# Stores of k and v straight from 32x32 blocks that VectorE has turned

## What is computed

```python
proj = xn @ w_in
u_a, z_a, q, k, v, z_b, g_a, g_b = jnp.split(proj, SPLITS, axis=-1)
y_a, h_last = s5_scan(u_a, h0, A_re, A_im, log_dt, B_re, B_im, C_re, C_im, D)
q = q.reshape(b, L, SB_HEADS, SB_HEAD_DIM)
k = k.reshape(b, L, SB_HEADS, SB_HEAD_DIM)
v = v.reshape(b, L, SB_HEADS, SB_HEAD_DIM)
o = sb_sweep(q, k_all, v_all, q_pos, k_pos, sb_bias).reshape(b, L, SB_WIDTH) * jax.nn.silu(z_b)
merged = jax.nn.sigmoid(g_a) * (y_a @ w_branch_a) + jax.nn.sigmoid(g_b) * (o @ w_branch_b)
return x + merged @ w_out, k, v, h_last
```

## Time and profile before

| | |
|---|---|
| median of the runs | 2971.93 us (2971.42 to 2975.23, 3 runs) |
| profiled execution, first to last instruction (span) | 2972.2 us; no other time of that execution is given |
| TensorE busy | 2927.0 us, 98% |
| VectorE busy | 1367.9 us, 46% |
| ScalarE busy | 1026.9 us, 35% |
| GpSimd busy | 433.7 us, 15% |
| mean granted clock of TensorE | 0.995 |
| DMA packets | 426099, of which 65122 under 512 bytes |

### The profile page before, as it was taken

The page is one execution under the profiler, slowest core; times in us unless marked ns, Lnnn a source line. Parts: engine busy times, 40 slices in busy tenths (PEclk is TensorE's granted clock), DMA queues, the critical chain, the costliest instruction groups (busy, mean ns, idle before and its releaser), DMA issues.

```text
span 2972.2 us, 48716 instructions
## 1 busy us (share of the span) xinstructions
PE 2927.0 (98%) x19148; PEld 2900.2 (98%) x19148; DVE 1367.9 (46%) x2579; ACT 1026.9 (35%) x1251; POOL 433.7 (15%) x1119
## 2 busy tenths in 40 slices
PE   6999999999999999999999999999999999999998
PEld 5999999999999999999999999999999999999997
DVE  6624453462445345244435524534566534422266
ACT  6235225423522541352253145125422421211242
POOL 7500330230032033004203300510000000000000
PEclk8999999999999999999999999999999999999999
DMA  6332332233233223323322331332448754332283
GB/s 185 84 107 70 85 90 88 74 92 104 65 93 99 84 67 89 100 65 99 105 72 71 92 106 52 103 100 72 150 154 300 244 189 138 114 112 71 82 244 114
DMA packets 426099, 329.05 MB, mean 111 GB/s; under 512 B 65122, under 2 KB 388274, under 8 KB 423858
## 3 DMA queue, kind: packets, MB, share of 16 engines
q1 hardware_dynamic: 425906, 326.34, 36.6%
HBM read 235.72 MB, written 73.73 MB: 104 GB/s over the span
## 4 chain that ended last, share of the span: by engine, by line
PE 90%; DMA 3%; SPq 2%; DVE 2%; ACT 1%; issue 1%; DVEq 0%; ACTq 0%
PE acc L1842 81%; PE side L1985 2%; PE side L2000 2%; DMA w_raw<-in_w_branch_a 1%; PE side L1809 1%; PE side L1980 1%; DMA t_sig_ga<-work 1%; PE side L1941 1%; SPq L522 0%; DMA work<-work 0%; PE side L1942 0%; PE side L2101 0%; DMA t_u_new<-work 0%; SPq L500 0%; DMA work<-in_x_prompt 0%
## 5 line engine op out<-in xcount | busy, mean ns | idle before, releaser
L1842 PE MATMUL acc<-x_high,w_high 128*128 128x344 f32 (+2 forms) x5440 | 1761.3, 324 | 3.8 <-DVE x_low L1421 2.0
L1842 PE MATMUL acc<-x_high,w_low 128*128 128x344 f32 (+2 forms) x5440 | 1734.6, 319 | 0.0
L1842 PE MATMUL acc<-x_low,w_high 128*128 128x344 f32 (+2 forms) x5440 | 1734.6, 319 | 0.0
L1842 PEld LDWEIGHTS acc<-x_high,w_high 128*128 128x128 f32 x5440 | 1023.4, 188 | 6.8 <-DVE x_low L1421 2.2
L1842 PEld LDWEIGHTS acc<-x_low,w_high 128*128 128x128 f32 x5440 | 1023.5, 188 | 1.0
L1842 PEld LDWEIGHTS acc<-x_high,w_low 128*128 128x128 f32 x5440 | 1022.4, 188 | 0.0
L1406 DVE TENSOR_TENSOR w_low<-w_raw,w_high 128x1024 fp32r<-128x1024 f32 x233 | 288.5, 1238 | 567.0 <-ACT w_high L930 564.3
L930 ACT CAST w_high<-w_raw 128x1024 fp32r<-128x1024 f32 x232 | 242.6, 1046 | 882.6 <-PE acc L1842 790.2
L1282 POOL COPY work<-s_tables 128x28 f32 x16 | 3.3, 206 | 1460.5 <-DVE work L1559 1208.3
L1559 DVE TENSOR_TENSOR work<-work,side 128x128 f32<-128x128 f32 x64 | 18.4, 287 | 319.9 <-PE side L1985 319.9
L986 ACT ACTIVATE work<-work 128x128 f32<-128x128 f32 (+3 forms) x64 | 43.9, 686 | 160.4 <-DVE work L1567 160.2
(11 more groups left out here) (320 smaller groups left out, 2560.0 us busy)
## 6 DMA issues: line engine op xcount, KB each, us to landing
w_raw<-in_w_in SPq DMA_DIRECT2D x160, 512.0 KB, 3.9
w_raw<-in_w_out SPq DMA_DIRECT2D x48, 512.0 KB, 4.0
work<-t_sig_ga SPq DMA_DIRECT2D x24, 516.0 KB, 4.0
out<-work SPq DMA_DIRECT2D x18, 512.0 KB
t_qk<-stage SPq DMA_DIRECT2D x16, 516.0 KB, 5.0
work<-t_qk SPq DMA_DIRECT2D x16, 516.0 KB, 4.7
t_sig_gb<-stage SPq DMA_DIRECT2D x16, 516.0 KB, 4.2
t_sig_ga<-stage SPq DMA_DIRECT2D x16, 516.0 KB, 4.7
```

The lines of the kernel that those rows point to most:

```text
L1842: ins = mm(acc[s][:, a, 0:n], w[b][:, kk, :], x[:, kx, c0:c0 + n], start=start, stop=stop)
```

## The change

Two instructions of VectorE turn k and v inside their stage buffers, each 32x32 block by itself (`V.transpose`). Afterwards partition 32q + a of block j holds features 32q to 32q + 31 of token 32j + a. `rows_out` stores that in four transfers, one for each q, each with 1024 runs of 32 floats (128 bytes), and the eight new tokens' columns in a fifth as 1024 single elements. The stores of k are issued in chunk 7, behind the second half's block loads, those of v in chunk 9. For q, ScalarE copies the eight new tokens' columns alone, and SyncE stores them as 1024 single elements in place of the tile. `attn_load` becomes one load, of v's rows, 512 bytes each, back from `v_prompt`. TensorE's three groups of transposes go, with their copies; the scores of the first block of queries wait for the load instead. The scratch tensor `t_qk` goes.

```diff
-                if t == Q:
-
-                    sp.wait_ge(at_in, i * 48 + PRIMED)
-                dst = {ZA: lambda: t_sza[bass.ds(i, 1)], Q: lambda: t_qk[0:1], K: lambda: t_qk[1:2], GB0: lambda: t_sgb[bass.ds(2 * i, 1)],
+                if t == Q:
+                    sp.dma_start(t_qs[:, bass.ds(i * P, P)].rearrange("b d -> d b"), stage[s][:, SEQ:TOK], allow_slow_non_contiguous=True).then_inc(stage_sent[s], 16)
+                    return
...
-                sp.wait_ge(stage_sent[0], i * 48 + 16 + PRIMED)
-                sp.wait_ge(stage_sent[1], i * 64 + 16 + PRIMED)
-                for n, dst in enumerate((qT, kT)):
-                    sp.dma_start(dst, t_qk[n]).then_inc(at_in, 16)
-                sp.wait_ge(stage_ready[0], i * 4 + 2 + PRIMED)
-                sp.dma_start(vT, stage[0][:, :]).then_inc(at_in, 16)
+                sp.wait_ge(kv_sent, i * 80 + 80 + PRIMED)
+                sp.dma_start(vtok.rearrange("p (b d) -> p b d", b=8),
+                             v_prompt[0, 0].rearrange("(b p) h d -> p b h d", p=P)[:, :, bass.ds(i, 1), :].rearrange("p b h d -> p b (h d)")).then_inc(at_in, 16)
+
+            def rows_out(turned, buf, rows, new, done):
+
+                sp.wait_ge(turned, i + 1)
+                for q in range(4):
+                    sp.dma_start(rows[0, 0][:, bass.ds(i, 1), q * 32:(q + 1) * 32].rearrange("(j a) h d -> a j (h d)", a=32),
+                                 buf[q * 32:(q + 1) * 32, 0:SEQ].rearrange("a (j d) -> a j d", d=32)).then_inc(done, 16)
+                sp.dma_start(new[0, :, 0, bass.ds(i, 1), :].rearrange("b h d -> (h d) b"), buf[:, SEQ:TOK], allow_slow_non_contiguous=True).then_inc(done, 16)
...
                 if cn == 7:
                     toeplitz(1)
+                    rows_out(k_turned, stage[1], k_prompt, k_sample, stage_sent[1])
+                if cn == 9:
+                    rows_out(v_turned, stage[0], v_prompt, v_sample, kv_sent)
...
-                if cn == 13:
-                    rows_out(vtok_ready, vtok, v_prompt)
-                    new_out()
-                if cn == 15:
-                    rows_out(ktok_ready, ktok, k_prompt)
...
-    VT, NTR, KTR, ZB_AT = 45, 46, 57, 44
+    K_TURN, V_TURN, ZB_AT = 26, 34, 44
...
             if t in (Q, K, V):
-                nc.scalar.copy(tok3(stage[s][:, :]), acc_v(t % 2)).then_inc(stage_ready[s], 1)
+                if t == Q:
+                    nc.scalar.copy(stage[s][:, SEQ:TOK], acc[t % 2][:, NB - 1, NC - NEW:NC]).then_inc(stage_ready[s], 1)
+                else:
+                    nc.scalar.copy(tok3(stage[s][:, :]), acc_v(t % 2)).then_inc(stage_ready[s], 1)
...
-                if p == KTR:
-                    dve.wait_ge(k_tr, i + 1)
-                    V.tensor_copy(ktok, side_flat).then_inc(ktok_ready, 1)
+                if p == K_TURN:
+                    dve.wait_ge(stage_ready[1], i * 4 + 1 + PRIMED)
+                    V.transpose(stage[1][:, 0:SEQ], stage[1][:, 0:SEQ]).then_inc(k_turned, 1)
+                if p == V_TURN:
+                    dve.wait_ge(stage_ready[0], i * 4 + 2 + PRIMED)
+                    V.transpose(stage[0][:, 0:SEQ], stage[0][:, 0:SEQ]).then_inc(v_turned, 1)
...
-                if p == VT:
-                    pe.wait_ge(at_in, i * 48 + 48 + PRIMED)
-                    pe.wait_ge(yt_ready, 2 * i + 2)
-                    for kb in range(8):
-                        last_op = tr(side_flat[:, kb * P:(kb + 1) * P], vT[:, kb * P:(kb + 1) * P], ident[:, :])
-                    last_op.then_inc(v_tr, 1)
-                if p == KTR:
-                    pe.wait_ge(z_ready, 8 * i + 4)
-                    for kb in range(8):
-                        last_op = tr(side_flat[:, kb * P:(kb + 1) * P], kT[:, kb * P:(kb + 1) * P], ident[:, :])
-                    last_op.then_inc(k_tr, 1)
-                if p == NTR:
-                    pe.wait_ge(vtok_ready, i + 1)
-                    for n, src in enumerate((qT, kT, vT)):
-                        last_op = tr(side[0:NEW, 0, n * P:(n + 1) * P], src[:, SEQ:TOK], ident[:, :])
-                    last_op.then_inc(new_tr, 1)
...
                         if qb == 0:
-                            pe.wait_ge(new_ready, i + 1)
+                            pe.wait_ge(at_in, i * 16 + 16 + PRIMED)
+                            pe.wait_ge(yt_ready, 2 * i + 2)
```

More of the change, by code:

```diff
@@ L227, in build @@
     c = Carve(work)
-    qT, kT, vT = c.take(TOK), c.take(TOK), c.take(TOK)
-    wT = vT[:, 0:SEQ]
+    c.at = 2 * TOK
+    wT = c.take(SEQ)
+    c.at = 3 * TOK
     vtok = c.take(SEQ)
     zb = [c.take(SEQ) for _ in range(2)]
-    ktok = c.take(SEQ)
+    c.at += SEQ
     lk, rl = c.take(SEQ), c.take(SEQ)
     szb = c.take(TOK)
-    smp = c.take(3 * P, NEW)
     c = Carve(work)
@@ L306, in build @@
         ("s5_hn_ready", "s5_ys_mm", "s5_ys_ready", "s5_yt_mm", "s5_yt_ready", "s5_y_sent", "s5_state_sent")]
-    at_in, v_tr, vtok_ready, k_tr, ktok_ready, new_tr, new_ready, kv_sent = [sem(s) for s in
-        ("attn_in", "v_tr", "vtok_ready", "k_tr", "ktok_ready", "new_tr", "new_ready", "kv_sent")]
+    at_in, k_turned, v_turned, kv_sent = [sem(s) for s in ("values_in", "k_turned", "v_turned", "v_sent")]
     sc_mm, z_ready, lr_ready, l_ready, arg_ready, w_ready, w_tr, wt_ready, pv_mm, oz_ready, oz_sent, szb_ready = [sem(s) for s in
@@ L363, in acc_v, with sent_before @@
         return acc[s][:, 0:banks, 0:n]
+    SENT = (48, 128)
+    def sent_before(t):
+        s, m = stage_of(t)
+        return 64 + 16 * m if s == 1 and m else 16 * m
     def tok3(ap):
@@ L573, in phase_a @@
                 ahead(cn)
-                if cn % 2 == 1 and cn > 1 and cn // 2 - 1 not in (U, V, ZB, GA0)[0:4 if last else 3]:
+                if cn % 2 == 1 and cn > 1 and cn // 2 - 1 not in (U, K, V, ZB, GA0)[0:5 if last else 4]:
                     send(cn // 2 - 1)
@@ L1011, in _ @@
             if f < 2:
[L1012 removed]
+                act.wait_ge(stage_sent[f], FT * SENT[f] + PRIMED)
             else:
```

31 lines of the change are left out of this document (6 added, 25 removed).

## The result

| | median, us | runs | ratio to before, 95% interval |
|---|---|---|---|
| before | 2972.41 | 2971.42 to 2975.23 | |
| after | 3204.57 | 3192.93 to 3211.89 | 1.0772 [1.0757, 1.0786] |
| forecast | 2955.5 (2952 to 2990) | | |

The change made the kernel 7.7% slower; the forecast said 0.6% faster, and its range did not hold the time. The profiled execution of after spans 3196.2 us, at a mean granted clock of 0.968.

The account below looks back on a forecast made before the run. TensorE, busy 2927.0 of 2972.2 us, was taken to bound the kernel. Removing 2.07 us of transposes in each of eight passes, with no stall, gave -16.6 us: 2955.5 us, range 2952 to 2990.

Parts of the forecast that it names:

- the landing of the swap: First swap of scan halves, queued behind k's stores, second pass: lands at 418.2 us, limit 419.2, so no stall.
- t: Time per packet of the short stores on the DMA queue: taken as 16 ns, bounds 9.4 and 47 ns.
- are cheaper than it up to 32 ns each: q's 1024 element stores, replacing a 516 KB store: claimed cheaper than that store up to 32 ns per element.
- The low bound: Low end of packet time for short stores: 9.4 ns from single-element loads, 10.4 ns from 64-byte loads; gives no stall.
- The term of the gain: Transposes taken off TensorE in the projection loop: 2.07 us per pass, 16.6 us over eight passes.
- The stores of rows: k's 128-byte runs on the DMA queue: 256 packets per engine, at 16 ns each, leaving 1.0 us before a stall.
- The readback of v: Load of v's rows before the scores: lands by 453.2 us, wanted at 460.8, 7.6 us to spare, cost nothing.
- Rival 1: Short stores at 32 ns delay the swap; TensorE waits 4.1 us per pass at step 36; 2988 us; chance 0.26.
- Rival 2: Stores at 23 to 27 ns; the stall gives back the transposes' gain; 2966 to 2976 us; chance 0.10.
- rival 4: VectorE's and ScalarE's score chain sets the pace of steps 47 to 79; removed work gives nothing; 2972 us; chance 0.03.
- Rival 3: v's readback lands late for the scores; 2 us beyond the margin leaves no gain, 2972 us; chance 0.03.
- The row I named for "wrong": Sign against the forecast: TensorE idle before step 36, released by VectorE, 4 us per pass or more; short packets above 25 ns.

Follow-up runs that it names:

- experiment 7: Changed kernel with q's and v's new tokens stored as 32-byte runs and k's 1024 elements sent to SBUF instead of memory: 2960.53 us, ratio 0.9948.
- experiment 1: Changed kernel with the three single-element stores of new tokens written as 128 runs of 32 bytes, in another order: 2958.67 us, ratio 0.9948.
- experiment 6: Changed kernel, q's and v's new tokens in 32-byte runs, k's store made 1024 runs of 32 bytes, 512 bytes apart in scratch: 2960.07 us, ratio 0.9950.
- experiment 8: Changed kernel with the same three element stores moved later, to groups 13, 15 and 17, from a small tile: 2967.01 us, ratio 0.9972.
- experiment 3: Kernel before, complete, with three stores per pass of 1024 single elements to scratch added at groups 5, 7 and 9: 3202.64 us, ratio 1.0768.

## Why the prediction was wrong

**The step that failed** is the landing of the swap, 409.7 + 0.32 t + 1.8 + 0.3 + 1.3, and with it the sentence on q, "are cheaper than it up to 32 ns each". Both price a store by the time its packets hold the engines. t was on the safe side: 13.0 to 13.7 ns for the rows and 9.2 ns for the elements, both below the 16 ns I took. (The 23 ns I read from the earlier trace rows for the 256-byte store was a misreading: the trace has 60 packets of 256 bytes there at 16 ns each, and 60 of 4 bytes that also took time.) By that formula there was no stall. But the 1.3 us from the last packet to the end, and the 28 ns for each packet behind, came from rows in which no element store stands ahead. Behind one, the packets took 363 ns and the swap 18.00 us. The 32 ns for q have no row of their own either, and q's store cost by a path that the prediction did not have at all, ScalarE starting 6.7 us after its product.

**The low bound was from the wrong rows.** Of the element stores held only the loads. A load of single elements writes into SBUF, and experiment 7 shows that this is cheap; none of the rows I read had many short writes that share a place in the memory. That is an operation the trace does not show, with a price for its packets only. I noted that for the 128-byte runs, and took the elements in with them, as part of one t. Their price should have been bounded apart, and for what stands behind them too.

The Trainium skill has the sentence that I should have weighed. "DMA: Bandwidth & Descriptors", Anatomy of one DMA — SWDGE (gpsimd) path, says of a transfer issued by GpSimd that the semaphore update is ordered behind the data write, which "can cause a surprisingly long delay especially when the write target is HBM". The transfers here are issued by SyncE, and no row shows when an element store's own semaphore fires, so the trace does not test that sentence. What it shows agrees in kind only: the same writes of 4 bytes, 8 bytes apart, cost 7.1 us per pass into DRAM and 0.2 us into SBUF. How long a delay can be, or that writes close together bring it, that section does not say.

The Trainium skill's page "VectorE: DVE Perf Modes", The three transpose paths, warns of a plain DMA that transposes by access pattern when the innermost stride of the destination is large. It compares with another way of transposing that no run here uses, so its factor is not tested. Among the runs here the large stride was not what cost: 64 or 512 bytes from one element to the next were nearly free (0.6 to 0.9 us per pass), 4 bytes cost 9.2 us per pass and more. What is slow here is many writes close together.

**The term of the gain was right.** The pass of experiment 1 is 257.64 - 255.57 = 2.07 us shorter, the 2.07 us I read from the earlier trace rows; the match to the last digit is chance. On the medians the gain is 15.4 us (2958.67 against 2974.09 for the kernel before in the same session), where I had 16.6: the forecast is good for the change without its element stores.

**The transposes on VectorE** took 1.23 us, as taken. **The stores of rows** were priced well. Experiment 1 begins its second pass 2.31 us earlier than before did (313.04 against 315.35), so its swap at 416.82 us is 419.1 us on the clock of the earlier trace rows; I had computed 418.2, and 419.2 as the limit. In this pass the margin was 0.3 us instead of 1.0, and it held; it failed in one other pass, by 0.2 us. VectorE waited 4.27 us for it, within the 2 to 5 us foretold.

**The readback of v** was no cost in experiment 1, where TensorE enters the scores without a wait. In after it is a cost, 19.2 us of waiting in all, because v's element store goes ahead of the y blocks and the readback.

**Rival 1** had the right sign and the right place for k, the product of step 36 waiting for VectorE; 86.3 of the 173 us of waits stand there. Its mechanism is out: short stores were not at 32 ns. The Trainium skill's rule that ended there ("DMA: Bandwidth & Descriptors", Specifications: below 512 bytes the engine reads, modifies and writes) did not show as a price for 128-byte runs (13.0 ns a packet, and no loss in experiment 1), nor for runs of 32 bytes (experiment 6). Whether it has a part in the delay by writes that share a place, no run tells. Rival 2 and rival 4 did not occur. Rival 3 occurred, by another mechanism, the element store of v. The row I named for "wrong" came, TensorE idle before step 36 with VectorE as its releaser; the packets above 25 ns came too, but they were the loads behind the store, not its own.

**The clock** was in no term. A stall costs more than its idle time: of the 239.2 us some 41 us, by the estimate above, are matmuls at the lower clock after TensorE had stood still.

## What to carry to other kernels

A store costs what its packets take, and then what it adds to the transfers that follow it; read a store's price from the landing of the next transfer, not from its own packets. Do not let many writes of a few bytes fill the same few dozen bytes of DRAM: turn the data on chip first, or write runs of 32 bytes or more. If such a store cannot be avoided, put it where only transfers that are needed late follow it, as in experiment 8, which gave back 238 us of the loss with the same three stores. And an empty stretch of the queue is no sign of a slow queue before it is known that something had been issued.

## What the hardware showed that was not expected

- 1024 writes of 4 bytes, 16 to each 64 bytes, had packets of 9.2 ns and slowed the 512-byte packets behind them from 28 to 363 ns for some 12 us. In experiment 8 such a store slowed a chunk that was issued 9.2 us after it.
- The same 1024 elements cost 0.8 us per pass 64 bytes apart, 1.6 us 16 bytes apart, 9.2 us without gaps, 15.0 us in rows 4 KB apart and 24.5 us in rows 16 KB apart; to SBUF, 8 bytes apart, they cost 0.2 us, where the same arrangement in DRAM cost 7.1 us.
- 8192 stores of 128 bytes per pass cost nothing that showed, at 13.0 ns per packet.
- With the element stores of q and v there are gaps that no releaser in the profile explains: ScalarE starts 6.7 us after its product behind q's store, and TensorE has 35.9 us in all ("issue") in after, 42.6 us in experiment 3 and 1.8 us in experiment 8. In the kernels with k's element store alone TensorE has none. A packet of the instruction queue ran at 409 us, when ScalarE went on; that instruction loads were held up would fit, and it was not tested.
